# Padding the split activations of a two-layer decoder by 32 bytes a part

## What is computed

```python
def conformer_mixer(h, w_in, conv_w, conv_b, ln_g, ln_b, w_out):
    a, b, z = split(h @ w_in, 3)                 # 2048 -> 3 * 2048
    u = a * sigmoid(b)
    c = causal_depthwise_conv(u, conv_w, 31) + conv_b
    y = silu(layernorm(c) * ln_g + ln_b) * silu(z)
    return y @ w_out                             # 2048 -> 2048

x = x + conformer_mixer(rmsnorm(x, a_norm), ...)
kv = rmsnorm(x, kv_norm) @ w_kv                  # 2048 -> 6 * 2048
q012_z = rmsnorm(x, b_norm) @ b_w_in             # 2048 -> 4 * 2048
x = x + (merge of three dilated attentions(q, k, v) * silu(z)) @ b_w_out
return rmsnorm(x, final_norm)
```

## Time and profile before

| | value |
|---|---|
| median of 3 runs | 1532.41 us |
| the profiled execution's own time | 1529.53 us |
| its span, first to last instruction | 1527.7 us |
| TensorE matmul busy (PE) | 1484.1 us, 97% |
| TensorE weight load busy (PEld, beside PE) | 1440.6 us, 94% |
| VectorE (DVE) | 797.0 us, 52% |
| ScalarE (ACT) | 689.1 us, 45% |
| GpSimd (POOL) | 387.0 us, 25% |
| HBM, over the span | 175 GB/s |
| mean granted TensorE clock | 0.997 of full speed |

### The profile page before, as it was taken

The page is one execution under the profiler, slowest core; times in us unless marked ns, Lnnn a source line. Parts: engine busy times, 40 slices in busy tenths (PEclk is TensorE's granted clock), DMA queues, the critical chain, the costliest instruction groups (busy, mean ns, idle before and its releaser), DMA issues.

```text
span 1527.7 us, 28300 instructions
## 1 busy us (share of the span) xinstructions
PE 1484.1 (97%) x11478; PEld 1440.6 (94%) x11478; DVE 797.0 (52%) x1190; ACT 689.1 (45%) x989; POOL 387.0 (25%) x168
## 2 busy tenths in 40 slices
PE   6999999979899999999999999999999999999997
PEld 5999999968799999999999999999999999999886
DVE  3799999570464444544444544445444454444333
ACT  5333343564564443544434444344444444434543
POOL 4888888668400000000000000000000000000595
PEclk9999999999999999999999999999999999999999
DMA  9666666445497666656666566665665666654652
GB/s 257 170 186 175 188 184 179 139 138 194 129 284 203 176 175 170 177 159 179 175 173 181 153 184 175 174 175 156 184 175 165 175 166 174 175 165 120 234 201 89
DMA packets 454141, 268.52 MB, mean 176 GB/s; under 512 B 4353, under 2 KB 436481, under 8 KB 453426
## 3 DMA queue, kind: packets, MB, share of 16 engines
q1 hardware_dynamic: 454098, 267.99, 61.2%
q10 hardware_dynamic: 6, 0.02, 0.0%
HBM read 263.71 MB, written 4.29 MB: 175 GB/s over the span
## 4 chain that ended last, share of the span: by engine, by line
issue 76%; POOL 18%; PE 5%; POOLq 0%; DVE 0%; ACT 0%
POOL w_lo L270 18%; PE bank L306 2%; PE bank L308 2%; PE bank L307 2%; POOLq L269 0%; ACT bank L680 0%; DVE y L964 0%; DVE resid L948 0%; PE bank L1108 0%; ACT y L701 0%; PE bank L326 0%; PE bank L325 0%; PE bank L324 0%; PE bank L1110 0%; ACT stat L696 0%
## 5 line engine op out<-in xcount | busy, mean ns | idle before, releaser
L261 ACT ACTIVATE w_hi<-raw 128x1024 fp32r<-128x1024 f32 x480 | 506.7, 1058 | 479.1 <-PE bank L288 397.4
L270 POOL TENSOR_TENSOR w_lo<-raw,w_hi 128x1024 fp32r<-128x1024 f32 x160 | 386.0, 2419 | 1124.5 <-ACT w_hi L261 1124.4
L286 PE MATMUL bank<-act_a,w_hi 128*128 128x256 f32 x2304 | 655.6, 285 | 5.3 <-DVE act_b L868 2.4
L288 PE MATMUL bank<-act_a,w_lo 128*128 128x256 f32 x2304 | 652.0, 283 | 0.0
L287 PE MATMUL bank<-act_a,w_hi 128*128 128x256 f32 x2304 | 651.9, 283 | 0.0
L270 DVE TENSOR_TENSOR w_lo<-raw,w_hi 128x1024 fp32r<-128x1024 f32 x320 | 391.5, 1229 | 498.2 <-ACT w_hi L261 498.2
L286 PEld LDWEIGHTS bank<-act_a,w_hi 128*128 128x128 f32 x2304 | 442.1, 192 | 7.2 <-DVE act_b L868 2.6
L287 PEld LDWEIGHTS bank<-act_a,w_hi 128*128 128x128 f32 x2304 | 442.3, 192 | 0.1
L288 PEld LDWEIGHTS bank<-act_a,w_lo 128*128 128x128 f32 x2304 | 442.2, 192 | 0.0
L286 PE MATMUL bank<-act_b,w_hi 128*128 128x256 f32 x1024 | 291.0, 284 | 0.0
L288 PE MATMUL bank<-act_b,w_lo 128*128 128x256 f32 x1024 | 289.7, 283 | 0.0
(11 more groups left out here) (119 smaller groups left out, 768.2 us busy)
## 6 DMA issues: line engine op xcount, KB each, us to landing
raw<-w_kv_dram SPq DMA_DIRECT2D x96, 1024.0 KB, 5.9
raw<-b_w_in_dram SPq DMA_DIRECT2D x64, 1024.0 KB, 6.6
raw<-a_w_in_dram SPq DMA_DIRECT2D x48, 1024.0 KB, 5.8
raw<-a_w_out_dram SPq DMA_DIRECT2D x16, 1024.0 KB, 5.1
raw<-b_w_out_dram SPq DMA_DIRECT2D x16, 1024.0 KB, 5.1
bias<-bias_dram SPq DMA_DIRECT2D x16, 384.0 KB, 8.0
x_sb<-x_dram SPq DMA_DIRECT2D x2, 1024.0 KB, 7.1
resid_dram<-x_sb SPq DMA_DIRECT2D x1, 2048.0 KB, 7.7
```

Source lines behind the costliest of these rows:

```text
L261: nc.scalar.activation(w_hi[:, stream.half_slot(half), :], raw[:, slot, part:part + HALF], ACT.Copy).then_inc(hi_done, 1)
L270: eng.tensor_tensor(w_lo[:, stream.half_slot(half), :], raw[:, slot, part:part + HALF], w_hi[:, stream.half_slot(half), :].bitcast(F32), A ...
L286: nc.tensor.matmul(dst[:, 0:S], wide_hi, source[:, kt, 0, :], start=(kt == 0), stop=False)
L288: mm = nc.tensor.matmul(dst[:, 0:S], wide_lo, source[:, kt, 0, :], start=False, stop=(kt == KT - 1))
```

## The change

Both activation tensors are allocated with 264 values in a part in place of 256 and used through a view of the first 256. Every reader and writer goes through that view. A part still holds 1024 bytes in one piece, and the next begins 1056 bytes behind it: part number i (two for each channel tile, high before low) begins 32 x i bytes further, modulo 512, than it did before. High parts stand at even multiples of 32 and low parts at odd ones. Each tensor is 1 KB longer in a partition (16 x 2 x 32 bytes), so what lies behind it moves by 1 KB or 2 KB. Weights stay where they are. No instruction is added, removed or moved, and no wait is changed.

```diff
+ACT_PAD = 8
...
-        act_a = sb("act_a", [P, KT, 2, S], F32R)
+        act_a = sb("act_a", [P, KT, 2, S + ACT_PAD], F32R)[:, :, :, 0:S]
...
-        act_b = sb("act_b", [P, KT, 2, S], F32R)
+        act_b = sb("act_b", [P, KT, 2, S + ACT_PAD], F32R)[:, :, :, 0:S]
```

## The result

The changed kernel takes 1511.62 us, the median of 4 runs (1510.1 to 1512.57), against 1532.25 us for the kernel before on the same chip (4 runs). The ratio is 0.9863, 95% interval 0.9846 to 0.9880: faster by 20.6 us. The forecast was no change. The time lies inside the stated range, at the end where the rival "faster, a little" had put it.

What follows compares the result with a forecast made beforehand. TensorE's distance between matmul starts was taken as the bound. All four terms were taken as 0, so the profiled 1529.53 us stayed, and the median of runs, 2.9 us higher, gave 1532.4 us; range 1504 to 1546 us.

Steps and rivals of the forecast that it cites:

- faster, a little: Moving stream and weight load meet in memory in a bad phase; shifting starts prevent settling: -14 us, 1518 us; chance 0.24.
- What bounds the kernel: In the heads and layer 0's input projections, the distance between matmul starts sets the pace, not loads or splits.
- Item 1, moving reads: Activation reads of `project` from shifted starts, 9984 matmuls: taken as 0, bounded by -98 and +33 us.
- d = 0: Price change per moving read in `project`, taken as none; 1 ns a matmul would be 10 us.
- The piece of 13.3 ns: Part of each matmul's start distance that does not grow with columns; 133 us over 9984 matmuls of 256 columns.
- The bounds: Limits for moving reads: -9.8 ns each, as in plain float32 passes, or +3.3 ns for one extra 32-byte piece.
- Item 2, stationary reads: Output projections' 768 weight loads from shifted places: taken as 0; 2.5 us cost if uncovered, 7.5 us gain at most.
- Items 3 and 4: Part writes and re-reads at four seams, 0.9 us at most, taken 0; shift of later buffers by 1 or 2 KB, 0.
- The others would keep up: In the large-gain rival (1427 us; below 1504 chance 0.09): GpSimd needs 2.40 us a half slab, 24 matmuls take 2.64.
- Signs in the profile: Expected afterwards if right: starts in a slab 120 ns apart for high and low parts, heads' stretch still 984 us.
- the case that the streams meet: Profile sign: distance differs by channel tile, period eight tiles; L287's median durations leave 283 ns for matmuls, 192 for loads.

## Where the prediction was right and where it was wrong

The time, 1511.6 us, lies in the range of 1504 to 1546, but the sum that gave the forecast held no gain at all. The range reached so far down only because it took in the rival "faster, a little" up to twice its price. So the range was right and the mechanism chosen was not.

**What bounds the kernel: right.** Where TensorE's distances shrank with nothing else in the way, in the heads, the time followed them: 23.7 of 24.6 us.

**Item 1, moving reads, is the step that failed.** It took d = 0, a fixed piece that knows no addresses, and the runs show a mean of -3.2 ns by addresses alone. Its two arguments were these. The piece of 13.3 ns is the same with 256 and 512 moving columns; that is so, but it does not mean that addresses are no part of it, since all operands of both shapes stood in the same relation. Over all relations tried the piece is 6.6 to 13.3 ns in the one shape and 13.4 to 20 in the other. And the 120 ns were even whatever other engines did; also so, but what matters is the place of TensorE's own other operand, and no other engine. The bounds were sound: -98 us and +33 us, with 113.3 ns the best that was met, two thirds of the way down to a plain float32 pass.

**The rival "faster, a little" was right in mechanism as far as the runs reach, and mis-sized.** That addresses decide is shown; that the streams meet in memory is not, it fits. It named the weight load, the bad phase and the distances of 118.6 ns behind an interruption; priced at 1.4 ns it gave 1518 us; the mean gain was 3.2 ns and 1511.6 us were measured. Its reason, that a start which shifts cannot settle, holds in part only: steps of 256 bytes change nothing, and constant shifts alone give means of 116.5 to 119.3 ns at every relation tried but 0 and 96, and 113.3 ns in one kernel. The kernel before stood at one of the two worst of the places tried, 0 (96 is the other).

**Item 2, stationary reads: wrong in sign and over its bound.** I took 0, covered by 227 ns, and allowed 2.5 us of cost. It costs 6.2 ns x 768 = 4.8 us. That a load has 227 ns until the next one does not cover it: the distance between matmuls grows all the same. Undoing this part shows it (4.7 us less of span).

**Items 3 and 4: nothing speaks against them.** The writes of layer 0's input keep their medians of 474 and 520 ns. The four stretches are accounted for within 1 us by distances and, in layer 0, by the wait and the lower clock.

**"The others would keep up" was wrong for layer 0.** The rival checked GpSimd's 2.40 of 2.88 us and not VectorE's 224 of 249, which stood among the rows. Nearly all of the 7.7 us was lost there, shown by the equal start of the output projection: 3.1 us went into the longer wait for VectorE, about 2 into the lower clock behind it, and the rest into smaller waits. The kernel with padding in the heads alone agrees, within 2 us.

**Signs in the profile.** A distance that differs by channel tile, medians of 279 and 188 ns: as named for the case that the streams meet. The period is four tiles, not eight.

By the Trainium skill's page "SBUF — State Buffer", section "Who interferes with whom", TensorE never waits for anyone and the sum would be 0. The runs disagree: the places of TensorE's own two operands change the distance by up to 6.7 ns a matmul. Between different engines no run here contradicts it.

**Open.** What meets what inside the memory, and why modulo 256, was not measured. Nor is it shown what sets the entry into 113 or 118 ns: each change lies behind plain float32 matmuls or a pause, but half of the pauses change nothing. Whether all of a head's slabs can be brought to 113 ns stays open too; by the count that would be about 10 us more.

## What to carry to other kernels

If matmuls stand further apart than their columns explain, compare where the streaming operand and the stationary one begin, modulo 256 bytes, and try a few relations for each shape: here 0 was, with 96, the worst place for streaming activations and the best for standing ones. Measure distances slab by slab, since one relation can have two steady distances and a mean hides them. Before pricing a faster engine, read every other engine's busy time in the same stretch: what the next one can't follow is not gained. Read the granted clock behind every wait that grows, too.

## What the runs showed of the hardware

- The distance of one-pass float matmuls with 256 columns was 120.0 ns at relation 0 and 113.3 or 117.8 ns at -64 bytes; with 512 columns 227 ns at relation 0 and 232 to 233 ns at the three others tried (32, 64, 128). It depends on where the two operands of TensorE begin relative to each other, modulo 256 bytes as far as tried.
- At one relation two distances (113.3 and 117.8 ns) stay constant over whole slabs of 48 matmuls. Plain float32 work in between can change one into the other, and so can a pause of 0.34 to 0.9 us from start to start with no matmul in it.
- In the middle of layer 0 TensorE waits for the sum over channels, and the granted clock can fall to its lower level there. Behind a wait of 2.2 us it stayed up in the kernel before and in the one with padding in the heads alone, and fell for 3.4 us in the ones with layer 0 at 256 bytes and with parts stepping by 256 bytes. Behind 5.2 us, in the changed kernel and in the one with unpadded output projections, it fell for 6.8 us. A spell of 3.4 us cost 1.5 us over four slabs, one of 6.8 us about 2 us in the slab behind the wait. This is one reason why the starts of the output projection differ by 1 to 4 us where layer 0 is at 120.0 ns.
